# Router logits taken inside the output projection, the gather buffer moved, and the expert loop's unused rounds put at its start

## The reference, cut to what matters

```python
mix = jnp.concatenate([o_h, o_s], axis=-1) @ w_o
x  = layer_norm(ALPHA * x + g1 * mix, ln1_g, ln1_b)
u2 = x * (1 + sc2) + sh2
x  = layer_norm(ALPHA * x + g2 * hier_moe(u2, ...), ln2_g, ln2_b)

def hier_moe(h, ...):                       # h: 288 x 2048
    g_logits = h @ w_gr + b_gr              # 4 groups
    e_logits = h @ w_er + b_er              # 4 x 8 experts
    # best group (weight: its softmax probability), in it the two best experts
    # (softmax over the two), each expert: (silu(h @ w_gate) * (h @ w_up)) @ w_down, width 512
```

## Time and profile before

| | |
|---|---|
| time, median of 3 runs | 1793.2 us (1792.18 to 1794.33) |
| the profiled execution's own time | 1794.54 us, of it span 1792.8 us |
| PE, DVE, ACT, POOL busy | 89%, 30%, 11%, 5% of the span |
| mean granted PE clock | 0.949 |
| moved by DMA | 536.94 MB, mean 300 GB/s |

### The profile page before, as it was taken

The page is one execution under the profiler, slowest core; times in us unless marked ns, Lnnn a source line. Parts: engine busy times, 40 slices in busy tenths (PEclk is TensorE's granted clock), DMA queues, the critical chain, the costliest instruction groups (busy, mean ns, idle before and its releaser), DMA issues.

```text
span 1792.8 us, 24828 instructions
## 1 busy us (share of the span) xinstructions
PE 1597.2 (89%) x9533; PEld 911.7 (51%) x9533; DVE 533.9 (30%) x922; ACT 195.0 (11%) x325; POOL 94.7 (5%) x172
## 2 busy tenths in 40 slices
PE   3679999999999999899967999999989888898992
PEld 0036666534777775477745545454434434344440
DVE  0010009731222222532245232323223232232325
ACT  0000001200000012430025010000010000100001
POOL 3000000000110100010001000000000000000000
PEclk8789999999989989899987999999999999999996
DMA  9998888876433444274334999999999999999971
GB/s 350 421 398 328 311 322 315 317 289 248 143 124 107 139 156 171 73 288 164 141 118 152 369 407 415 402 421 420 409 401 415 404 403 410 401 421 412 413 327 53
DMA packets 79391, 536.94 MB, mean 300 GB/s; under 512 B 10386, under 2 KB 10562, under 8 KB 18066
## 3 DMA queue, kind: packets, MB, share of 16 engines
q1 hardware_dynamic: 72146, 507.62, 71.1%
q0 software_dynamic: 6576, 26.35, 4.7%
q10 hardware_dynamic: 624, 2.36, 0.3%
HBM read 533.40 MB, written 11.80 MB: 304 GB/s over the span
## 4 chain that ended last, share of the span: by engine, by line
PE 69%; DMA 18%; DVE 5%; SPq 4%; issue 2%; ACT 1%; DVEq 0%; ACTq 0%
PE ps L579 18%; DMA ring<-w_gate 13%; PE ps L1085 13%; PE ps L923 7%; PE ps L592 6%; PE ps L1105 5%; DMA ring<-w_ada 5%; PE ps L563 4%; SPq L373 4%; PE ps L1067 3%; DVE arena L1869 1%; PE ps L1031 1%; PE ps L735 1%; PE ps L1073 1%; PE ps L716 1%
## 5 line engine op out<-in xcount | busy, mean ns | idle before, releaser
L1085 PE MATMUL ps<-ring,arena 128*64 128x256 f32 x3200 | 357.6, 382 | 19.0 <-DMA ring<-w_gate 19.0
L579 PE MATMUL ps<-arena,ring 128*128 128x288 f32 x1280 | 322.3, 410 | 0.0
L1085 PEld LDWEIGHTS ps<-ring,arena 128*64 128x64 f32 x3200 | 226.5, 137 | 165.9 <-DMA ring<-w_gate 34.9
L579 PEld LDWEIGHTS ps<-arena,ring 128*128 128x128 f32 x1280 | 240.9, 191 | 89.6 <-issue 25.1
L1105 PE MATMUL ps<-arena 128*64 128x512 f32 x800 | 181.0, 598 | 31.0 <-DMA arena<-w_down 18.1
L563 PE MATMUL ps<-ring,silu_c 128*32 128x512 f32 x768 | 114.6, 706 | 54.6 <-DMA ring<-w_ada 28.2
L1105 PEld LDWEIGHTS ps<-arena 128*64 128x64 f32 x800 | 53.6, 136 | 142.4 <-issue 85.4
L1067 PE MATMUL ps<-arena 64*128 64x512 f32 x400 | 111.4, 649 | 15.3 <-DVE arena L1869 12.8
L923 PE MATMUL ps<-arena,ring 128*128 128x288 f32 x512 | 124.7, 406 | 0.0
L592 PE MATMUL ps<-ring,arena 128*128 128x512 f32 x256 | 116.6, 604 | 1.3 <-ACT arena L1147 0.7
L923 PEld LDWEIGHTS ps<-arena,ring 128*128 128x128 f32 x512 | 97.2, 190 | 26.8
(11 more groups left out here) (421 smaller groups left out, 1198.4 us busy)
## 6 DMA issues: line engine op xcount, KB each, us to landing
ring<-w_gate SPq DMA_DIRECT2D x100, 1024.0 KB, 24.2
ring<-w_up SPq DMA_DIRECT2D x100, 1024.0 KB, 26.6
arena<-w_down SPq DMA_DIRECT2D x100, 1024.0 KB, 26.9
ring<-w_ada SPq DMA_DIRECT2D x96, 1024.0 KB, 8.8
ring<-w_in SPq DMA_DIRECT2D x56, 1024.0 KB, 6.3
ring<-w_o SPq DMA_DIRECT2D x16, 1024.0 KB, 5.8
ring<-cache_k SPq DMA_DIRECT2D x16, 512.0 KB, 3.8
ring<-cache_v SPq DMA_DIRECT2D x16, 512.0 KB, 3.9
```

The costliest lines, as they stand in the source:

```text
L579: last = mm(ps[:, bank, 0:T], ring[:, slot, P * t:P * (t + 1)], uT[:, t, :], start=(t == 0), stop=(t == KC - 1))
L1085: last = mm(ps[B * s:B * (s + 1), 2 + c // 4, 0:256], xgT[:, 4 * (c % 4) + t, :], ring[:, c, 512 * t + 256 * s:512 * t + 256 * (s + 1)], s ...
```

## The change

**The logits.** A layer norm is linear but for the mean and the reciprocal root of a token, and both are the same for all features. So the logits can be had from `rT` before the norm: `rstd * (W(gain*r) - mean * W(gain)) + W(offset)`. ACT and DVE write `gain*r` of each slice to a small buffer `rg[m % 4]`, with 18 more columns for gain and offset of the 9 sequences (`gain_sample`), and PE multiplies it with the router's weights two slices behind the projection (`logit_part`). The even slices go to one part of a PSUM bank, the odd ones to another. DVE puts the logits together between the first `centre` and the second; the 16 matmuls behind the norm go. The three small instructions on `adaT` (lines 1738 to 1741) move ahead of the projection.

**The turns.** PE no longer waits for logits before it turns `u2T`; it takes the four slices of a group for both prompt tiles as soon as they are there, and the logits behind the fourth step.

**The gather buffer** moves to where the first tile of token rows (`urow[0]`) was, so it is free when these rows are stored.

**The loop.** `If(i < nblocks)` becomes `If(n + nblocks >= NBLK)` with `i = (n + nblocks + 24) % 64`, on all five engines: the 40 - nblocks rounds without work come first. `turn_rows(1)` goes from between the two parts of `spread_columns` into the first round with work.

```diff
-        xg = area(4608, D, parts=B)
+        xg = area(16384, D, parts=B)
 # sync
-            with sp.Fori(1, NBLK) as i:
-                with sp.If(i < nblocks):
+            with sp.Fori(1, NBLK) as n:
+                with sp.If(n + nblocks > NBLK):
+                    i = nc.s_assert_within(sp.snap((n + nblocks + (64 - NBLK)) % 64), 0, NBLK - 1,
...
 # gpsimd
+            pool.wait_ge(u2_first, 16)
+            link(g.memset(xg, 0.0))
             pool.wait_ge(plan_ready, 1)
...
-            pool.wait_ge(u2_act, KC)
-            pool.wait_ge(x1_act, KC)
-            pool.wait_ge(tt_pe, 24)
-            link(g.memset(xg, 0.0))
             pool.wait_ge(idx_made, 1)
             nc.gpsimd.tensor_copy(idx1[:], idxs[:, 0:1]).then_inc(idx_ready, 1)
             gather(1)
+            pool.wait_ge(tt_pe, 24)
...
 # tensor
+            def logit_part(m):
+
+                pe.wait_ge(rg_act, m + 1)
+                pe.wait_ge(rg_dve, m + 1)
+                lo = B * (m % 2)
+                mm(ps[lo:lo + NL, 0, 0:NW], wr[:, m, :], rg[m % 4], start=(m < 2), stop=(m >= KC - 2)
+                   ).then_inc(lp_pe, 1)
...
                 wo_half(m, 1)
+                if m >= 2:
+                    logit_part(m - 2)
+            logit_part(KC - 2)
+            logit_part(KC - 1)
...
-            for m in range(KC):
-                pe.wait_ge(u2_act, m + 1)
-                if m == 0:
-                    pe.wait_ge(u2_dve, 1)
-                last = mm(ps[0:NL, 4, 0:T], wr[:, m, :], u2T[:, m, :], start=(m == 0), stop=(m == KC - 1))
-            last.then_inc(rt_pe, 1)
...
+            for x in range(8):
+                i, q = x % 2, x // 2
+                pe.wait_ge(u2_act, 4 * q + 4)
+                turn_tokens(x, i, q, u2T)
+                if x == 3:
+                    pe.wait_ge(lg_dve, 2)
+                    for j, (t0, tn) in enumerate(TILES):
+                        last = nc.tensor.transpose(ps[0:tn, 5, 64 * j:64 * j + NL], lgT[:, t0:t0 + tn],
+                                                   ident[0:NL, 0:NL])
+                    last.then_inc(rt_pe, 1)
...
             pe.wait_ge(g2_act, 3)
-            turn_rows(1)
             pe.wait_ge(diag_ready, 2)
             spread_columns((2, 3)).then_inc(where_pe, 1)
...
-            with pe.Fori(0, NBLK) as i:
-                with pe.If(i < nblocks):
+            with pe.Fori(0, NBLK) as n:
+                with pe.If(n + nblocks >= NBLK):
+                    i = nc.s_assert_within(pe.snap((n + nblocks + (64 - NBLK)) % 64), 0, NBLK - 1,
+                                           skip_runtime_bounds_check_because="the branch holds it there")
+                    with pe.If(i < 1):
+                        turn_rows(1)
                     pe.wait_ge(x_copied, i + 1)
...
 # scalar
                 A(r2[m % 4], rT[:, m, :], ACT.Square).then_inc(wo_act, 1)
+                if m >= 4:
+                    act.wait_ge(lp_pe, m - 3)
+                A(rg[m % 4][:, 0:TP], rT[:, m, 0:TP], ACT.Copy, scale=adaT[:, 4, m, 0:1]).then_inc(rg_act, 1)
...
 # vector
+            def gain_sample(m):
+
+                dve.wait_ge(wo_dve, m + 1)
+                if m >= 4:
+                    dve.wait_ge(lp_pe, m - 3)
+                v.tensor_copy(rg[m % 4][:, T:NW].rearrange("p (i r) -> p i r", r=R), adaT[:, 3:5, m, :])
+                v.tensor_tensor(rg[m % 4][:, TP:T].rearrange("p (b t) -> p b t", t=SS),
+                                rT[:, m, TP:T].rearrange("p (b t) -> p b t", t=SS), seq(adaT[:, 4, m, 1:R]),
+                                ALU.mult).then_inc(rg_dve, 1)
...
+                if m >= 1:
+                    gain_sample(m - 1)
                 if m >= 2:
                     add_sums(m - 1)
+            gain_sample(KC - 1)
             add_sums(KC - 1)
...
+            dve.wait_ge(lp_pe, KC)
+            v.tensor_copy(lgs, ps[0:NL, 0, 0:NW])
             centre(0)
...
             scale_rows(0)
+            link(v.tensor_tensor(lgT, lgs[:, 0:T], lgT, ALU.subtract))
+            link(v.tensor_tensor(lgT, lgT, rstd[0:NL, :], ALU.mult))
```

106 lines of the change are left out of this document (63 added, 43 removed).

## The result

The changed kernel takes 1805.36 us (median of 5, 1802.28 to 1806.62), the kernel before 1793.2 (median of 5) on the same chip: ratio 1.0054, 95% interval 1.0043 to 1.0065, that is 9.7 us slower (7.7 to 11.7). The two medians themselves lie 12.2 us apart, the two profiled spans 12.0, and the same kernel executed again later stands 9.3 us above the kernel before beside it (1804.90 and 1795.63): the difference is 9 to 12 us by whichever of them. Forecast were 1795 and a range of 1788 to 1799.5, so the time lies outside it. The profiled execution took 1806.62 us with a span of 1804.8, 12.0 more than the span before.

What follows compares the result with a forecast made beforehand. Weight loads were taken to bound the expert stage, PE close under. Exit -6.7 and entry with all before it +8.7 made +2.0 us: 1796.5 for the profiled execution, median 1795 against 1793.2, range 1788 to 1799.5.

Steps and rivals of the forecast that it cites:

- The exit: Behind the last block: no empty rounds left, DVE waits last for ACT's table load and copies; -6.7 us.
- The stage: The 25 expert blocks: paced by weight loads, length unchanged, starting with the first gate matmul; earlier delays shift its end.
- The projection: Output projection on PE: thirteen logit matmuls at 0.515 us each ahead of the last slice's end; +6.7 us.
- Norm, routing and the clock: From projection to loop: logits moved, DVE 2.35 us later, turns starting at low clock; +1.3 us net including projection (-0.3 to +2.8).
- The entry: Column spread to first gate matmul: PE's empty rounds partly show; +8.7 us with all before it, +5.5 to +12.0.
- all that lead: PE's sequencer reaching the entry's loop up to 5.3 us ahead of its matmuls, so rounds end at 989.3.
- rival B: Clearly slower: sequencer not ahead at entry, low clock through the turns, dearer register instruction; +5.3 us, 1798.5, chance 0.25.
- The rounds: Empty rounds' price on PE, from the idle time at the exit: 9.98 / 15 = 0.67 us each.
- Rival C: Faster: PE's empty rounds cost about 0.41 us as on ACT, the rest stays hidden at exit; -4.5 us, 1788.7, chance 0.25.

Runs made afterwards that it cites:

- loop_only: The kernel before with the loop's change alone (conditions, `i`, place of `turn_rows(1)`); ratio 1.0014 to the kernel before, +2.5 us.
- after_short_body: The changed kernel with a 25-round working loop and, on PE ahead of it, 15 rounds jumping over one never-taken semaphore increment; ratio 0.998 to the kernel before.

## Why the prediction failed

**The exit: right.** -6.7 forecast, -6.6 found, by the mechanism named: not PE's combine but ACT's table load and copies release DVE last.

**The stage: right.** Its length stayed, what comes before it shifts the end, and the empty rounds of ACT, POOL (6.28 us) and DVE are hidden.

**The projection: the mechanism right, the size wrong.** The step "A logit matmul has 306 columns for 288: 0.515 us" went by passes and took the weight load as hidden. It measured 0.84 each, 10.83 us for 6.7, +4.1. Columns were the right price for 100 weight columns (0.515), not for 36.

**Norm, routing and the clock: somewhat better than forecast.** Behind the projection the change was to give 1.3 - 6.7 = -5.4 us up to the loop, and gave -6.78. PE began the turns low, as taken, and rose at 954, when its first four steps and most of two more were done. Together with the projection the way to the spread costs +4.05 where 1.3 was forecast, and so lies outside the range of -0.3 to +2.8 of that step.

**The entry: wrong, 12.59 us for 7.4, in two steps.** "If it uses all that lead ... 989.3; if no more than at the exit ... 992.7. I take 991.0": it used no more than at the exit. loop_only idles 10.01 us behind the spread, where before had 9.98 behind the last block, so that bound was the value, and the middle between the two had nothing behind it: +1.7. The Trainium skill, TensorE: Matmul & The Clock Gate, section on engine queue depths, has 64 instructions in TensorE's queue; no trace here shows a lead of that size at a loop that starts with a taken branch: the rounds start 1.1 to 1.2 us ahead at both ends. What the table of packets adds is that in loop_only the code was on its way 3.9 us ahead of the spread's end, so the sequencer had come to the branch by then, and that 2.7 us passed from there to the first round (13.94 - 11.2). So it seems to have been the code and not the sequencer's place that kept the lead small; no run takes this wait away and leaves the rounds.

The other 2.8 us, 3.3 in the first trace, were in no step: the gather's earlier end was counted as a gain alone, and what is queued behind it on POOL, ln2's transfers, was not followed. They move onto the time in which PE's sequencer needs new code. That a branch needs code was in no step either, though the rows of the instruction queues stood on the page of before.

It is the rival B in size (+5.3 forecast at its far end, +9.7 found). Of B's reasons the sequencer that is no further ahead than at the exit (992.7) held; the lower clock through all turns did not; and a round costs 0.75 us with the register instruction at the entry and 0.74 without it at the exit, so that instruction doesn't show.

**The miss in all.** Together the steps account for the miss: projection +4.1, norm and routing -1.4, entry +5.2, exit +0.1, stage +0.4 and the projection's later start +1.6 make the 10 us between the 2.0 of the forecast and the 12.0 of the spans.

**The rounds: the price was too low, the sum nearly right.** 0.67 us (9.98 / 15) took the idle time for the rounds; ten rounds removed give 0.74 to 0.75, and the lead is the difference. Rival C's 0.41 to 0.43 holds for ACT and POOL alone. C was also summed up wrongly: 6.1 us of rounds end at 982.7 + 6.1 + 1.9 - 5.3 = 985.4 with all the lead and at 988.8 with none, not "no later than 984.4", so its 1788.7 should have been 1789.7 or more. The 108 ns for a compare-and-branch in the Trainium skill, Advanced Engine Details and Errata, Control Flow Timing, would make 3.2 us for 15 rounds of two; after_short_body leaves room for that with a short body (idle 1.13 us), but over the long body the trace has 11.2.

**Shown and not shown.** Shown by runs: 0.75 us a round, the home's 2.8 us and ln2 as its cause, 0.32 us that go with narrow weights, the pair at the price of one. Only argued: that the packet is the code behind the body, for which the first jump waits, and that it also kept the lead in loop_only small. Open: why a jump over a long body takes up to 0.6 us.

## What to carry to other kernels

Rounds that do nothing are not free, and moving them does not make them cheaper: at the exit they lay partly beside another engine's work, at the entry beside nothing. Nest them in groups first. When a wait goes away, follow each instruction that was queued behind it: here a gather that ended sooner let 2.6 MB go just when the matrix engine's sequencer needed code. And a matmul with few weight columns between wide ones is not priced by its passes alone; look at the weight loads on both sides of it, and put two with different output rows next to each other.

## What was not expected of the hardware

- Two matmuls with 36 weight columns each, to output rows 0 to 35 and 64 to 99, ran in the time of one: four passes of 306 columns in 0.71 us, 0.84 us out of the projection for one and for two.
- Narrow weights between wide ones leave the weight loads idle 0.39 and 0.49 us at the two switches; 100 columns for 36 removed both, and the matmul cost 0.515 us for 0.84.
- The 16 KB packet of code at the loop's first jump came 2.8 us later, counted from the spread's end, while 2.6 MB of other transfers were moving (DMA share 1.00 in the window shown); held back, they gave the 2.8 us of idle time back.
- An empty round cost 0.75 us on PE and 0.43 on ACT and POOL, and 0.22 more on PE when a comparison with a register took the place of an addition and a comparison with a constant.
